# Attention tiles placed between the q, k, v products and between the output projection's products, on one core

## What is computed

```python
qkv = xn @ w_qkv                                   # xn: 256 x 1024, w_qkv: 1024 x 3072
q, k, v = jnp.split(qkv, [QK_WIDTH, 2 * QK_WIDTH], axis=-1)
q = apply_rope(rms_norm(q, q_norm), cos, sin)      # 8 heads x 2 halves x 64
k = apply_rope(rms_norm(k, k_norm), cos, sin)
s = jnp.einsum('bqhcd,bkhcd->bhcqk', qb, kb) * ATTN_SCALE      # causal, blocks of 128 queries
a = jax.nn.softmax(s, axis=-1)
a = a[:, :, 0] - lam * a[:, :, 1]
o = rms_norm(einsum('bhqk,bkhe->bqhe', a, vb), subln_g) * (1.0 - lam_init)
return o.reshape(B, S, V_WIDTH) @ w_o
```

## Time and profile before

| | |
|---|---|
| time, median of 3 runs | 1496.54 us (1492.62 to 1496.6) |
| the profiled execution's own time | 1494.25 us |
| its span, first to last instruction | 1492.4 us |
| PE busy, share of the span | 96% |
| DVE, ACT, POOL busy | 77%, 62%, 9% |
| stage of the change | 18.2 to 196.7 us |
| mean granted TensorE clock | 0.974 |

### The profile page before, as it was taken

The page is one execution under the profiler, slowest core; times in us unless marked ns, Lnnn a source line. Parts: engine busy times, 40 slices in busy tenths (PEclk is TensorE's granted clock), DMA queues, the critical chain, the costliest instruction groups (busy, mean ns, idle before and its releaser), DMA issues.

```text
span 1492.4 us, 19671 instructions
## 1 busy us (share of the span) xinstructions
PE 1439.9 (96%) x7268; PEld 1203.7 (81%) x7268; DVE 1155.9 (77%) x894; ACT 928.4 (62%) x796; POOL 129.3 (9%) x129
## 2 busy tenths in 40 slices
PE   6899899999978999999999999999999999999998
PEld 5675699999777888888888888888888888888876
DVE  4775555545766888988988898898899889889885
ACT  4434444343445776777776777777777677777763
POOL 6650270000140000000000000000000000000000
PEclk9985899999999999999999999999999999999999
DMA  9450345555545989999999999999999999999970
GB/s 336 151 169 1 118 165 197 185 191 177 182 151 180 368 294 336 350 365 346 348 365 372 341 344 371 354 351 367 339 349 365 378 336 357 375 336 355 357 286 29
DMA packets 191374, 423.00 MB, mean 283 GB/s; under 512 B 6752, under 2 KB 30304, under 8 KB 191328
## 3 DMA queue, kind: packets, MB, share of 16 engines
q1 hardware_dynamic: 190880, 421.55, 78.6%
q0 software_dynamic: 448, 0.82, 0.3%
HBM read 421.30 MB, written 1.05 MB: 283 GB/s over the span
## 4 chain that ended last, share of the span: by engine, by line
PE 87%; DVE 6%; ACT 3%; POOL 2%; issue 1%; DMA 1%; SPq 0%; POOLq 0%; ACTq 0%; DVEq 0%
PE ps L264 26%; PE ps L266 26%; PE ps L265 26%; PE ps L732 2%; DVE w_lo L235 2%; PE ps L541 2%; PE ps L611 2%; POOL rstd L1477 1%; ACT w_hi L229 1%; PE ps L748 1%; DVE wide L1167 1%; DVE xs L1085 1%; DMA raw<-in_attn_w_qkv_dram 1%; PE ps L564 1%; ACT y_hi L1014 0%
## 5 line engine op out<-in xcount | busy, mean ns | idle before, releaser
L235 DVE TENSOR_TENSOR w_lo<-raw,w_hi 128x2048 fp32r<-128x2048 f32 (+1 forms) x393 | 880.8, 2256 | 210.5 <-ACT w_hi L229 210.1
L229 ACT ACTIVATE w_hi<-raw 128x2048 fp32r<-128x2048 f32 x393 | 752.0, 1916 | 202.2 <-PE ps L266 199.0
L264 PE MATMUL ps<-w_hi,xe_hi 128*128 128x512 f32 x896 | 355.6, 397 | 1.8 <-DVE w_lo L235 1.8
L266 PE MATMUL ps<-w_hi,xe_lo 128*128 128x512 f32 x896 | 349.7, 390 | 0.0
L265 PE MATMUL ps<-w_lo,xe_hi 128*128 128x512 f32 x896 | 349.5, 390 | 0.0
L264 PE MATMUL ps<-w_hi,h_t_hi 128*128 128x512 f32 x536 | 210.4, 393 | 3.4 <-DVE h_t_lo L1250 1.8
L266 PE MATMUL ps<-w_hi,h_t_lo 128*128 128x512 f32 x536 | 208.9, 390 | 0.0
L265 PE MATMUL ps<-w_lo,h_t_hi 128*128 128x512 f32 x536 | 208.7, 389 | 0.0
L264 PEld LDWEIGHTS ps<-w_hi,xe_hi 128*128 128x128 f32 x896 | 168.6, 188 | 38.1 <-DVE w_lo L235 5.0
L266 PEld LDWEIGHTS ps<-w_hi,xe_lo 128*128 128x128 f32 x896 | 168.5, 188 | 36.0
L265 PEld LDWEIGHTS ps<-w_lo,xe_hi 128*128 128x128 f32 x896 | 168.8, 188 | 33.3
(11 more groups left out here) (215 smaller groups left out, 1357.1 us busy)
## 6 DMA issues: line engine op xcount, KB each, us to landing
raw<-in_moe_w_gate_dram SPq DMA_DIRECT2D x112, 1024.0 KB, 6.9
raw<-in_moe_w_down_dram SPq DMA_DIRECT2D x111, 1024.0 KB, 6.7
raw<-in_moe_w_up_dram SPq DMA_DIRECT2D x110, 1024.0 KB, 6.9
raw<-in_attn_w_qkv_dram SPq DMA_DIRECT2D x12, 1024.0 KB, 15.7
raw<-in_ffn_w_gate_dram SPq DMA_DIRECT2D x11, 1024.0 KB, 5.3
raw<-in_ffn_w_up_dram SPq DMA_DIRECT2D x11, 1024.0 KB, 5.2
raw<-in_ffn_w_down_dram SPq DMA_DIRECT2D x11, 1024.0 KB, 4.8
raw<-in_ple_w_gate_dram SPq DMA_DIRECT2D x8, 1024.0 KB, 8.4
```

Source lines behind the costliest of these rows:

```text
L229: nc.scalar.activation(w_hi[:, u % SPLIT, :], raw_slot(u), ACT.Copy).then_inc(hi_ready, 1)
L235: nc.vector.tensor_tensor(w_lo[:, u % SPLIT, 0:n], raw_slot(u)[:, 0:n], w_hi[:, u % SPLIT, 0:n].bitcast(F32), ALU.subtract).then_inc(lo_re ...
L264: nc.tensor.matmul(out, x[0], w[0], start=first, stop=False)
L266: return nc.tensor.matmul(out, x[1], w[0], start=False, stop=last)
```

## The change

Q, k and v are made in blocks k 0-3, q 0-3, v 0-3, then k 4-7, q 4-7, v 4-7 (`block_at`). The first six units are made as before. In the second six, each of the 12 `tile512` products (k = 0 to 11 in the code) is followed by a piece of the attention of heads 0-3: `score`, `attend`, `transpose_probs`. Heads 4-7 follow; between their pieces stand the first half of the output projection in 16 granules (`wo_granule`, three matmuls each). `wo_second` is the other half.

A score is one matmul over all 128 rows: `k_pad` holds each head's k twice, once with the lower and once with the upper 64 rows zero, and POOL clears it first. Rotation works on a block of both token tiles, six operations on DVE and none on POOL. Q isn't normalized: its root goes into the scale of the exponentials. `softmax_end` has three operations for four. Units 8 to 15 leave `SHARED`, so DVE makes all of their rest. The small inputs go from POOL's queue to SP's. The squares of `resid` (norm 1) are taken tile by tile for half by half. Scratch tensors lie over others that are unused then.

```diff
-SHARED = (0, *range(2, 16), 56)
+SHARED = (0, *range(2, 8), 56)
@@ SP
+                    if u == 1:
+                        load_small()
+                    if u == 3:
+                        for layer in range(2):
+                            sp.dma_start(p_sb[:, layer],
+                                         dram["p"][layer, 0].rearrange("(t p) n -> p t n", p=P)).then_inc(p_landed, 16)
...
+        GRANULES = {8: 4, 9: 2, 10: 2, 12: 1, 14: 1, 15: 1, 16: 1, 17: 1}
...
-        QUARTERS = {0: BY_TILE, 1: BY_HALF, 2: BY_TILE, 3: BY_HALF, 4: BY_TILE, 5: BY_TILE}
+        QUARTERS = {0: BY_TILE, 1: BY_TILE, 2: BY_TILE, 3: BY_HALF, 4: BY_TILE, 5: BY_TILE}
@@ PE
+                if i >= 2:
+                    pe.wait_ge(exp_ready, 2 * (i - 1))
+                out = ps[:, bank, 0:2 * nk].rearrange("p (c n) -> p c n", c=2)
+                nc.tensor.matmul(out, q_t[:, h, qt * P:(qt + 1) * P], k_pad[:, h, :, 0:nk], start=True, stop=False)
+                nc.tensor.matmul(out[:, :, nk - P:nk], ident16[:, :], causal16[:, :].unsqueeze(1).to_broadcast([P, 2, P]),
+                                 start=False, stop=True).then_inc(scores_ready, 1)
...
+            for k in range(12):
+                b, half, tt = 3 + k // 4, (k % 4) // 2, k % 2
+                u = 2 * b + half
...
+                last = tile512(u, half, 2 * (b % 2) + tt, tt)
...
+                if k == 0:
+                    pe.wait_ge(qk_rotated, 2)
+                    pe.wait_ge(p_lo_ready, 2)
+                    transpose_heads(1, 6).then_inc(q_transposed, 1)
+                if 1 <= k < 9:
+                    score(k - 1)
+                if k >= 4:
+                    attend(k - 4)
+                if 3 <= k < 11:
+                    transpose_probs(k - 3)
...
+            for i in range(8, HEAD_TILES + 3):
                 if i < HEAD_TILES:
...
+                    score(i)
+                if i >= 11:
+                    attend(i - 3)
+                if i == 10:
+                    pe.wait_ge(av_copied, 2)
+                    transpose_o(1)
+                for _ in range(GRANULES.get(i, 0)):
+                    wo_granule(granule)
+                    granule += 1
+                if 10 <= i < HEAD_TILES + 2:
+                    transpose_probs(i - 2)
...
+            wo_second(0, 0)
+            pe.wait_ge(exp_ready, 2 * 16)
+            transpose_o(3)
+            wo_second(1, 0)
+            wo_second(0, 1)
+            wo_second(1, 1)
@@ ACT, behind head tile 15
+            split_hi(U_WO + 3)
+            turned_o_hi(3)
+            for u in range(U_WO + 2, U_FFN):
                 split_hi(u + AHEAD)
@@ DVE, behind head tile 15
+            o_means(3)
+            norm_o(3)
+            split_lo(U_WO + 3)
+            turned_o_lo(3)
+            for u in range(U_WO + 2, U_FFN):
                 split_lo(u + AHEAD)
...
+            for q in range(4):
+                tt, n = q // 2, q % 2
...
+                nc.vector.tensor_tensor(r, r, ps[:, q, :], ALU.add).then_inc(resid_ready, 1)
```

More of the change, by code:

```diff
@@ L128, in trunk @@
         more = sb("more", [P, 1], I32)
+        with nc.sbuf_tensor("o_scratch", [P, 512], F32) as o_scratch:
+            pass
         pick = sb("pick", [P, TT * SLOTS])
@@ new lines, in transpose_probs @@
+            def transpose_probs(j):
+                pe.wait_ge(probs_ready, j + 1)
+                if j:
+                    pe.wait_ge(probs_t_copied, j)
+                if j == 8:
+                    pe.wait_ge(o_lo_ready, 1)
+                for kc in range(keys_of(j) // P):
+                    last = nc.tensor.transpose(ps[:, 6, kc * P:(kc + 1) * P], probs[:, j % BUFS, kc * P:(kc + 1) * P],
+                                               ident[:, :])
+                last.then_inc(probs_transposed, 1)
@@ new lines, in attend @@
+            def attend(j):
+                h, nt, at = head_of(j), keys_of(j) // P, (j % 4) * P
+                pe.wait_ge(probs_t_copied, j + 1)
+                if j % 8 == 0:
+                    pe.wait_ge(block_copied, 3 * (j // 8 + 1))
+                if j % 4 == 0 and j:
+                    pe.wait_ge(av_copied, j // 4)
+                if j == 8:
+                    pe.wait_ge(o_lo_ready, 2)
+                for kc in range(nt):
+                    last = nc.tensor.matmul(ps[:, 7, at:at + P], probs_t[:, j % 2, kc * P:(kc + 1) * P],
+                                            qkv[:, kc, 2 * D + h * P:2 * D + (h + 1) * P], start=kc == 0, stop=kc == nt - 1)
+                last.then_inc(av_ready, 1)
@@ new lines, in wo_granule @@
+            def wo_granule(g):
+                tt, n, c = g // 8, (g // 4) % 2, g % 4
+                if g == 0:
+                    unit(U_WO)
+                    pe.wait_ge(k_top_copied, 2)
+                    pe.wait_ge(k_bottom_copied, 2)
+                if g == 4:
+                    unit(U_WO + 1)
+                if g % 8 == 0:
+                    pe.wait_ge(o_lo_ready, tt + 1)
+                if g == 8:
+                    pe.wait_ge(block_copied, 6)
+                last = product(ps[:, 2 * tt + n, :], acts(c, tt), weights(U_WO + n, c, 0, 512, 512), c == 0, False)
+                if tt == 1 and c == 3:
+                    last.then_inc(unit_used, 1)
@@ new lines, in _, with wo_second @@
+            while granule < 16:
+                wo_granule(granule)
+                granule += 1
+            def wo_second(n, tt):
+                unit(U_WO + 2 + n)
+                pe.wait_ge(o_lo_ready, 3 + tt)
+                tile512(U_WO + 2 + n, 1, 2 * tt + n, tt).then_inc(unit_used if tt else wo_ready, 1)
+            wo_second(0, 0)
[4 more added lines that the diff above has]
+            wo_second(1, 1)
@@ L880, in _, with turned_o_hi @@
+            def turned_o_hi(m):
+                act.wait_ge(o_transposed, m + 1)
+                nc.scalar.activation(quarter(a_hi, m % 2, m // 2), bank4(O_BANKS[m]), ACT.Copy,
+                                     scale=sub_gain[:, 0:1]).then_inc(o_hi_ready, 1)
+            for u in range(6):
+                split_hi(u + AHEAD)
+                if u == 2:
                     act.wait_ge(small_landed, 144)
@@ L1534, in _ @@
+            qk_root(3)
+            for m in range(1, 4):
+                o_root(m)
             norm_root(1)
```

636 lines of the change are left out of this document (342 added, 294 removed).

## The result

The changed kernel takes 1456.28 us (median of 4 runs, 1453.39 to 1457.46) against 1496.08 us for the kernel before, a ratio of 0.9736 [0.9714, 0.9758]. Measured again beside the experiments it was 1456.16 us, ratio 0.9744 [0.9731, 0.9758]. The profiled execution took 1453.39 us with a span of 1451.7. The forecast was 1459, the range 1448 to 1480.

What follows compares the result with a forecast made beforehand. PE was taken as the bound, at half clock in attention, with waits for POOL's rotation half. Stage terms put the dense start at 159.1 instead of 196.7; less 1.6 unlisted, 36 us gained: 1459 us, range 1448 to 1480.

Steps and rivals of the forecast that it cites:

- First six units: Start of the stage, 18.2 to 54.2 us: units and k's transposes set the time, k's rotation hides under them.
- I take nothing: Small inputs on SP's queue delay unit loads at no cost, given 11 us of cover; ends -0.5 and +3 us.
- Twelve tiles: Products with attention of heads 0-3, 54.2 to 102.4 us: 46.4 us of PE work plus waits of 0.6 and 1.2.
- the rival of 1470: Hand-written order stalls the middle: PE waits 0.6 to 1.2 us more in each of 12 steps; chance 0.15.
- Full clock in the middle: Among the twelve tiles the clock stays full, since products fill 60 to 70% and scores use 128 rows.
- The rival of a clock that is low from the first score on: Float32 scores pull the clock down even between products, middle PE work 46.4 becomes 93 us: 1523; chance 0.05.
- Heads 4-7: With 13 granules, 102.4 to 134.7 us: 32.3 us, bound by steps through three engines; ends 27 and 47.
- The rival of a low clock in the whole stretch: Heads 4-7 run at clock 0.50, taking 47 us instead of 32: 1474; chance 0.18.
- Second half of the projection: 134.7 to 147.0 us: four products of 2.74, transposes 0.4, and 0.9 waiting for unit 15's rest.
- Norm 1: Last product to dense stage: 6.9 plus 3.5 for the late ring, 10.4 us, plus 1.7 for a low-clock restart.
- DVE isn't the bound: In the middle DVE has 36 us of work in 48, including 8.6 us for eight units' whole rests.
- The rival that the gain doesn't arrive: A later stage, the experts' loads, takes the gain back: 1495; chance 0.04.

Runs made afterwards that it cites:

- r1_changed: The changed kernel measured again, unaltered, beside the later experiments: 1456.16 us, ratio 0.9744 to the kernel before.
- e8_inputs: The changed kernel with its small inputs and p issued from POOL's queue again instead of SP's: 1458.01 us, ratio 0.9752 to the kernel before.
- e1_seq: The changed kernel with the attention of heads 0-3 run behind the twelve product tiles instead of between them: 1465.7 us, ratio 0.9794 to the kernel before.
- e2_seq64: The changed kernel with attention of heads 0-3 behind the products and each score as two 64-row matmuls: 1486.26 us, ratio 0.9942 to the kernel before.
- e3_64rows: The changed kernel with each score as two 64-row matmuls, products and granules in between as before: 1469.01 us, ratio 0.9826 to the kernel before.
- e5_tail: The changed kernel with unit 17's split behind half the squares and its rest behind the additions and norm: 1449.71 us, ratio 0.9706 to the kernel before.
- e7_shared: The changed kernel with POOL making half of the rests of units 8 to 15 again: 1461.27 us, ratio 0.9776 to the kernel before.

## Why the prediction was right, step by step

*First six units (54.2 predicted, 52.0 measured).* The sum of units and transposes held. PE started 0.9 us earlier, which is the bound of -0.5 given for the small inputs, and a little more; and this profile has the clock at 1.00 from the first product, where in the kernel before it was 0.50 for some 3 us. Other profiles of changed kernels have 0.50 there too (r1_changed has 0.95 over the stretch instead of 1.00), so this part of 1.3 us is chance: in r1_changed the first six units end at 53.8, and the forecast for them is 0.4 off. "I take nothing" for SP's queue is borne out by e8_inputs, but the reason was incomplete. The cover of 11 us was there; what I hadn't seen is that lateness of units 2 and 3 shifts DVE's list against POOL's halves.

*Twelve tiles (48.2 predicted, 47.0 measured).* The terms off were the scores: 0.7 and 1.2 us predicted for 128 and 256 keys, 0.54 and 0.97 measured (59.94 and 85.90 to the start of the mask, plus 0.11 for it). That is 1.6 us over eight tiles. The extrapolation from rows 4 to four times the columns was too high; the lower bound, columns alone, was nearer. The two waits, 0.6 and 1.2 us, came as one of 1.5, ahead of the q transposes, for p's rest as foretold. Root and shared rest 7 on POOL cost PE nothing here, but narrowly: the rest ended at 60.17 and PE came for it at 60.39, where in e1_seq and e2_seq64 PE waited 1.24 and 1.74 us for it. And of the 0.6 to 1.2 us in each step (the rival of 1470) there is no trace: PE is busy for 45.05 of 46.9 us.

*Full clock in the middle.* The forecast rested on it, and e1_seq, e2_seq64 and e3_64rows bear the reasons out. The rival of a clock that is low from the first score on (1523) was rightly small. It would have needed 64-row scores and no products between them: that is e2_seq64, 1486. My reading of rows 5, that scores pull the clock down though PE is busy, was right, and the 128-row form was the reason to go by, whether by its rows or by its fewer, longer matmuls. By the Trainium skill's rule ("TensorE: Matmul & The Clock Gate", Part 4: PE-mode transpose), which I weighed there, the full clock does not engage for transposes. These traces don't agree: transposes are in all of these stretches, and the clock is 1.00 from 92 to 107 us in e1_seq and from 62 to 108 in e3_64rows. The row at 103.54 had said so.

*Heads 4-7 (32.3 predicted, 33.1 measured).* From 98.98 to the second half of the projection at 132.06. The first wait was exact (2.6 us, ninth score at 101.56). The wait for o's rest ended at 113.0, 14.0 us into the stretch where 13.3 had been forecast, and that is nearly all of the 0.8. Behind these 2.2 us without work the clock is at 0.55 on the mean from 114 to 117.8. It cost nothing: r1_changed had the same wait and kept 1.00, and from the ninth score to unit 15's product both take 35.00 us. The first line is the ninth score, the second unit 15's product, in r1_changed (in the changed kernel's profile 101.56 and 136.56):

```profile
103.44 0.70 PE L578 MATMUL ps<-k_pad,xs 128*128 128x256 f32 x2 [1.11 <-ACT xs L992]
...
138.44 0.50 PE L275 MATMUL ps<-w_hi,a_hi 128*128 128x512 f32 x1 [1.18 <-DVE w_lo L246]
```

So such a gap may cost the clock or not, and 3.8 us at half clock are hidden where the steps through three engines set the pace, as the prediction had it. The rival of a low clock in the whole stretch (1474) is what e3_64rows comes near to, with 1469. Its price was reckoned too low: 25 us of PE's work at half clock are 50 us, more than the 47 it was given.

*Second half of the projection (12.3 predicted, 12.7 measured).* The wait for unit 15's rest was 1.18 instead of 0.9.

*Norm 1 (10.4 plus 1.7 predicted, 10.8 measured).* From 144.8 to 155.6. The sequence was as foretold: unit 17's split, its rest, four additions, norm. The 1.7 for a restart at the low clock was wrong in its place. The clock was low for some 3 us on the norm's transposes, which mostly wait for others anyway, and the dense matmuls ran at 1.00. e5_tail confirms the term of 3.5 us by undoing it: 3.6 in the profile.

*The sum.* 159.1 was forecast for the dense start and 155.6 came: 2.2 from the first units, 1.2 from the middle, 1.3 from the restart, less 0.8 and 0.4. The 1.6 us taken off for steps not listed were not needed either. With r1_changed's 157.13 the difference is 2.0, 0.4 of it from the first units. The median is 2.7 below the forecast, inside the forecast's own 1452 to 1466. That DVE isn't the bound, with eight more whole rests, was right in its sign for a reason that I hadn't given: the prediction charged DVE with 8.6 us for giving up POOL's help, and by e7_shared giving it up was itself worth 5 us. This is the step I would call wrong, though it moved the sum little. I had seen the 2.79 us beside POOL and priced it for the rotation only.

*The rival that the gain doesn't arrive (1495)*: 41.2 us at the dense start, 40.7 at the end.

## What to carry to other kernels

When a stage is bound by PE at half clock, look at what the matmuls there are made of before looking at gaps: one matmul padded with zeros to 128 rows, in place of two over 64, was worth 20.6 us here with the first eight tiles behind one another, and 12.7 with products between them; a good part of both is the shorter form at full clock. Half an elementwise operation given to POOL relieves DVE of that half, but small operations that come behind it can wait for the whole of POOL's, and here that cost more than it saved: 3.6 us with units 2 to 7, 5.1 more with units 8 to 15. And where a ring gives way late, the split that waits for it belongs behind the short operations of the next step, in both engines' lists.

## What the runs showed of the hardware

- The granted clock doesn't go by busy time alone. With 64-row scores it fell to 0.50 behind 4 us in which PE was busy for 3.37; with 128-row scores it stayed at 1.00 behind 4 us with 2.78, and through 11 us with 8.7 (e2_seq64 and e1_seq, from 92 and 96 us). In the kernel before it was 0.50 with PE busy for 45.91 of 46 us.
- The clock falls after a stretch with little work, but not each time. In e1_seq it fell at about 107, after two microseconds in which PE was busy for 0.35 and 0.21 of each:

```profile
104.00:105.00 1.00, 0.35 (x3) 0.11 (x2) 0.90 (x4) 1.00 (x8) 0.00 (x0) 1.00 0.00 0
105.00:106.00 1.00, 0.21 (x1) 0.21 (x2) 0.81 (x3) 1.00 (x6) 0.06 (x1) 1.00 0.00 0
...
107.00:108.00 1.00, 0.81 (x4) 0.81 (x5) 0.93 (x4) 0.14 (x1) 1.00 (x1) 0.65 0.00 0
```

- POOL's half of a rest holds up DVE's operations with two inputs in SBUF, but POOL's root didn't: it ran from 36.10 to 39.39 in the changed kernel, and DVE's six rotation operations from 35.93 to 39.90 took 0.68 to 0.70 us each, as they do alone. Beside the half from 32.53 to 35.98 a `TENSOR_REDUCE` with one input (L1300) took 1.21 us, as alone, but a `TENSOR_SCALAR` on one tensor (L1255) 1.14, where 0.17 is the rule.
